# Post-norm with ScalarE's square root and one Newton step, the first side transposed inside the tail, and the S5 tables' sines and copies issued at other places

## The reference

```python
def rmsnorm(x, gain):
    xf = x.astype(jnp.float32)
    y = xf * lax.rsqrt(jnp.mean(xf * xf, axis=-1, keepdims=True) + EPS)
    return (y * gain.astype(jnp.float32)).astype(x.dtype)

    for i in range(DEPTH_2):                 # DEPTH_2 = 2, EPS = 1e-6
        h = rmsnorm(x, mix_pre_gain[i])
        m = fox_mixer(...) if i == 0 else s5_mixer(...)
        x = x + rmsnorm(m, mix_post_gain[i])
        h = rmsnorm(x, ffn_pre_gain[i])
        x = x + rmsnorm(swiglu(h, ffn_w_gate[i], ffn_w_up[i], ffn_w_down[i]), ffn_post_gain[i])
```

## Time and profile before

| | |
|---|---|
| time before, median of 3 runs | 1224.45 us (1222.07 to 1225.02) |
| the profiled execution: time, span | 1224.62 us, 1222.8 us |
| mean granted TensorE clock | 0.976 of full speed |
| PE busy | 1151.2 us, 94% of the span, 7172 instructions |
| DVE busy | 799.1 us, 65% |
| ACT busy | 593.1 us, 49% |
| POOL busy | 117.8 us, 10% |
| DMA | 177.43 MB, mean 145 GB/s |
| the chain that ended last | PE 76%, DVE 13%, ACT 7%, POOL 2% |

### The profile page before, as it was taken

The page is one execution under the profiler, slowest core; times in us unless marked ns, Lnnn a source line. Parts: engine busy times, 40 slices in busy tenths (PEclk is TensorE's granted clock), DMA queues, the critical chain, the costliest instruction groups (busy, mean ns, idle before and its releaser), DMA issues.

```text
span 1222.8 us, 17457 instructions
## 1 busy us (share of the span) xinstructions
PE 1151.2 (94%) x7172; PEld 949.6 (78%) x7172; DVE 799.1 (65%) x1299; ACT 593.1 (49%) x907; POOL 117.8 (10%) x120
## 2 busy tenths in 40 slices
PE   7898799999999999999998899999988898999997
PEld 6766688797888888888777777887877677888785
DVE  5647763547767768555667886778768958455643
ACT  6465322325356656356664664343582256435441
POOL 0304150400000000000000000002304400000000
PEclk9899799999999999999999999999998899999999
DMA  8533012113455555554422554555441143555551
GB/s 304 178 105 95 26 52 70 35 53 131 151 200 173 183 178 173 188 185 164 153 89 98 189 197 160 187 184 190 165 145 54 58 148 137 197 189 187 189 189 52
DMA packets 49664, 177.43 MB, mean 145 GB/s; under 512 B 5648, under 2 KB 6288, under 8 KB 49328
## 3 DMA queue, kind: packets, MB, share of 16 engines
q1 hardware_dynamic: 49584, 176.32, 42.6%
HBM read 175.25 MB, written 1.05 MB: 144 GB/s over the span
## 4 chain that ended last, share of the span: by engine, by line
PE 76%; DVE 13%; ACT 7%; POOL 2%; issue 2%; DMA 1%; SPq 0%; DVEq 0%; ACTq 0%
PE wps L2616 20%; PE wps L2618 20%; PE wps L2617 20%; PE tps L2605 4%; DVE wlo L1773 3%; ACT whi L1390 2%; PE tps L2817 2%; PE tps L2826 1%; PE tps L2839 1%; DVE bt L2379 1%; DVE bt L2390 1%; DVE arena L1998 1%; PE tps L2662 1%; PE tps L3012 1%; POOL arena L2509 1%
## 5 line engine op out<-in xcount | busy, mean ns | idle before, releaser
L1773 DVE TENSOR_TENSOR wlo<-raw,whi 128x1024 fp32r<-128x1024 f32 (+1 forms) x322 | 388.6, 1231 | 184.2 <-ACT whi L1390 182.9
L2616 PE MATMUL wps<-whi,a_hi 128*128 128x512 f32 (+1 forms) x1008 | 405.4, 402 | 19.0 <-DVE a_lo L1795 7.8
L2617 PE MATMUL wps<-whi,a_lo 128*128 128x512 f32 (+1 forms) x1008 | 395.4, 392 | 0.0
L2618 PE MATMUL wps<-wlo,a_hi 128*128 128x512 f32 (+1 forms) x1008 | 395.2, 392 | 0.0
L1390 ACT ACTIVATE whi<-raw 128x1024 fp32r<-128x1024 f32 (+1 forms) x322 | 325.3, 1050 | 53.1 <-PE wps L2618 48.8
L2616 PEld LDWEIGHTS wps<-whi,a_hi 128*128 128x128 f32 x1008 | 192.4, 191 | 64.5 <-DVE wlo L1773 13.8
L2618 PEld LDWEIGHTS wps<-wlo,a_hi 128*128 128x128 f32 x1008 | 192.0, 191 | 40.7
L2617 PEld LDWEIGHTS wps<-whi,a_lo 128*128 128x128 f32 x1008 | 192.5, 191 | 36.4
L2616 PE MATMUL wps<-whi,f_hi 128*128 128x512 f32 x264 | 104.8, 397 | 0.0
L2618 PE MATMUL wps<-wlo,f_hi 128*128 128x512 f32 x264 | 104.3, 395 | 0.0
L2617 PE MATMUL wps<-whi,f_lo 128*128 128x512 f32 x264 | 104.3, 395 | 0.0
(11 more groups left out here) (402 smaller groups left out, 1335.4 us busy)
## 6 DMA issues: line engine op xcount, KB each, us to landing
raw<-in_w_dn SPq DMA_DIRECT2D x22, 512.0 KB, 3.6
raw<-in_w_0dn SPq DMA_DIRECT2D x22, 512.0 KB, 3.6
raw<-in_w_1dn SPq DMA_DIRECT2D x22, 512.0 KB, 4.2
raw<-in_w_ua SPq DMA_DIRECT2D x20, 512.0 KB, 3.6
raw<-in_w_ub SPq DMA_DIRECT2D x20, 512.0 KB, 3.7
raw<-in_w_0ug SPq DMA_DIRECT2D x20, 512.0 KB, 3.6
raw<-in_w_0uu SPq DMA_DIRECT2D x20, 512.0 KB, 3.7
raw<-in_w_1ug SPq DMA_DIRECT2D x20, 512.0 KB, 3.7
```

Source lines behind the costliest of these rows:

```text
L1773: V.tensor_tensor(t.wlo[n % NR][:, 0:w], t.raw[n % NR][:, 0:w], t.whi[n % NH][:, 0:w].bitcast(F32), ALU.subtract).then_inc(m.done(s.dve_lo ...
L2616: T.matmul(o, xh, wh, start=first, stop=False)
L2617: T.matmul(o, xl, wh, start=False, stop=False)
L2618: mm = T.matmul(o, xh, wl, start=False, stop=last)
```

## The change

The post-norm's reciprocal square root is formed in another way. ACT computes the square root of the mean (the first half's sum comes in as a bias that DVE has prepared at place (0,1), the second half's sum is the input), DVE takes the reciprocal of it and does one Newton step. Beside it, an ACT square root of a constant is issued at (0,1), so that the table of the square root is loaded there. In each post-norm all squares now come ahead of the multiplications. Side 0 is turned behind (1,2), inside the tail of the second half's stream, and no longer behind the stream. `b_power` is emitted at one piece per slab from 12 slabs ahead of 0dn0 on, so `s5_angle` and what follows come earlier; the sines are emitted from slab 3 of 0dn0's on instead of 14; the three groups of copies `c_spread` are emitted at the end of the first 7 slabs of 0dn1, at place (0,0) of its tail, and in si0's stream; `local_weights` is spread over one more slab.

```diff
-    def postnorm(names, nk, acts, then=None, begun=None):
+    def postnorm(names, nk, acts, then=None, begun=None, beside_tail=lambda banks: None):
...
+        def biases(banks):
+            for j in range(2):
+                emit("post_bias", i, j)
...
-        banks = whole(stream(names[1], nk, acts, {(0, TAIL - 1): half_way}))
-        take_in(1, 1, banks, first)
+        banks = whole(stream(names[1], nk, acts, {(0, 0): beside_tail, (0, 1): biases, (0, TAIL - 1): half_way, (1, 2): lambda b_: first()}))
+        take_in(1, 1, banks)
...
                 emit("b_power", k, i)
                 yield
-                if at["use"] < down_slab:
+                if at["use"] < down_slab - 12:
                     yield
...
         emit("c_zero")
-        for k in range(3):
-            emit("c_spread", k)
-            yield
+        emit("c_spread", 0)
+
+    def last_spread():
+        emit("c_spread", 2)
+        yield
...
-    sine_slab, dead_slab = down_slab + 14, SLABS.index(("0dn1", 6, 512)) + 1
+    sine_slab, dead_slab = down_slab + 3, SLABS.index(("0dn1", 6, 512)) + 1
-    x4, second = swiglu(0, second, ("mix_pre", 8))
+    x4, second = swiglu(0, second, ("mix_pre", 8), beside_tail=lambda banks: emit("c_spread", 1))
...
                     k_bank[0].held = False
+            else:
+                yield
             yield
...
+    background.append(last_spread())
     background.append(local_weights())
...
     @part
+    def post_bias(i, j):
+        if j == 0:
+            act.wait_ge(*m.at("eps", 3))
+            activate(t.st[:, 54:55], t.eps[:, 0:1], ACT.Sqrt, bias=t.eps[:, 0:1], scale=1.0)...
+
+    @part
+    def post_root(i, j):
+        act.wait_ge(*m.at("post_square", i, 1, j))
+        act.wait_ge(*m.at("post_bias", i, j))
+        activate(t.st[:, 48 + j:49 + j], t.st[:, 41 + 2 * j:42 + 2 * j], ACT.Sqrt, bias=t.st[:, 50 + j:51 + j], scale=1.0 / D)...
...
+    def post_bias(i, j):
+        dve.wait_ge(*m.at("post_square", i, 0, j))
+        V.tensor_scalar(t.st[:, 50 + j:51 + j], t.st[:, 40 + 2 * j:41 + 2 * j], 1.0 / D, 1e-6, ALU.mult, ALU.add)...
...
     def post_root(i, j):
-        a = t.st[:, 44 + j:45 + j]
-        for c in range(2):
-            dve.wait_ge(*m.at("post_square", i, c, j))
+        a, xh, y, tt = (t.st[:, c + j:c + j + 1] for c in (44, 52, 48, 56))
+        dve.wait_ge(*m.at("post_square", i, 1, j))
         V.tensor_tensor(a, t.st[:, 40 + 2 * j:41 + 2 * j], t.st[:, 41 + 2 * j:42 + 2 * j], ALU.add)...
-        after_last()
-        rsqrt(t.st[:, 46 + j:47 + j], a, 1, 1.0 / D, 1e-6, "post_root", i, j)
+        V.tensor_scalar(xh, a, -0.5 / D, -0.5e-6, ALU.mult, ALU.add)...
+        dve.wait_ge(*m.at("post_sqrt", i, j))
+        V.reciprocal(y, y)...
+        V.scalar_tensor_tensor(tt, y, y, xh, ALU.mult, ALU.mult)...
+        V.scalar_tensor_tensor(t.st[:, 46 + j:47 + j], tt, 1.5, y, ALU.add, ALU.mult)...
```

More of the change, by code:

```diff
@@ L732, in postnorm, with take_in @@
         done = [[(("post", i, c, j),) for c in range(2)] for j in range(2)]
-        def take_in(c, j, banks, between=None):
+        def take_in(c, j, banks):
             b = banks[j]
[L736 to L744, removed]
+            emit("post_square", i, names[c], c, j, b.name)
+            emit("post_times", i, names[c], c, j, b.name)
+            b.free = (("post_times", i, c, j),)
         def close(j):
@@ L764, in postnorm, with swiglu @@
         return done, second
-    def swiglu(l, second, then=None):
+    def swiglu(l, second, then=None, **more):
         ffn = Acts(f"f{l + 1}")
@@ L791, in swiglu @@
         to_acts("sg1", [("gate_up", name, j) for j in range(2)], ffn, 2, k0=20)
-        return postnorm([f"{l}dn0", f"{l}dn1"], 22, ffn, then)
+        return postnorm([f"{l}dn0", f"{l}dn1"], 22, ffn, then, **more)
     emit("fox_start", x2_all)
@@ L1610, in post_square @@
         last_square[:] = [("post_square", i, c, j)]
+    @part
+    def post_bias(i, j):
+        if j == 0:
+            act.wait_ge(*m.at("eps", 3))
+            activate(t.st[:, 54:55], t.eps[:, 0:1], ACT.Sqrt, bias=t.eps[:, 0:1], scale=1.0).then_inc(m.done(s.act_out, "root_table", i), 1)
+    @part
+    def post_root(i, j):
+        act.wait_ge(*m.at("post_square", i, 1, j))
+        act.wait_ge(*m.at("post_bias", i, j))
+        activate(t.st[:, 48 + j:49 + j], t.st[:, 41 + 2 * j:42 + 2 * j], ACT.Sqrt, bias=t.st[:, 50 + j:51 + j], scale=1.0 / D).then_inc(
+            m.done(s.act_out, "post_sqrt", i, j), 1)
     @part
@@ L2131, in post_times @@
         dve.wait_ge(*m.at("post_gain", i))
-        if after_square:
-            dve.wait_ge(*m.at("post_square", i, c, j))
+        dve.wait_ge(*m.at("post_square", i, c, j))
         V.tensor_tensor(t.h[:, j, cols], t.bank[b][:, :], t.gain[:, cols], ALU.mult).then_inc(m.done(s.dve_out, "post_times", i, c, j), 1)
     @part
+    def post_bias(i, j):
+        dve.wait_ge(*m.at("post_square", i, 0, j))
+        V.tensor_scalar(t.st[:, 50 + j:51 + j], t.st[:, 40 + 2 * j:41 + 2 * j], 1.0 / D, 1e-6, ALU.mult, ALU.add).then_inc(
+            m.done(s.dve_out, "post_bias", i, j), 1)
+    @part
     def post_root(i, j):
-        a = t.st[:, 44 + j:45 + j]
-        for c in range(2):
-            dve.wait_ge(*m.at("post_square", i, c, j))
+        a, xh, y, tt = (t.st[:, c + j:c + j + 1] for c in (44, 52, 48, 56))
+        dve.wait_ge(*m.at("post_square", i, 1, j))
         V.tensor_tensor(a, t.st[:, 40 + 2 * j:41 + 2 * j], t.st[:, 41 + 2 * j:42 + 2 * j], ALU.add).then_inc(m.done(s.dve_out, "post_sum", i, j), 1)
-        after_last()
-        rsqrt(t.st[:, 46 + j:47 + j], a, 1, 1.0 / D, 1e-6, "post_root", i, j)
+        dve.wait_ge(*m.at("post_sum", i, j))
+        V.tensor_scalar(xh, a, -0.5 / D, -0.5e-6, ALU.mult, ALU.add).then_inc(m.done(s.dve_out, "post_half", i, j), 1)
+        dve.wait_ge(*m.at("post_sqrt", i, j))
+        V.reciprocal(y, y).then_inc(m.done(s.dve_out, "post_guess", i, j), 1)
+        dve.wait_ge(*m.at("post_guess", i, j))
+        V.scalar_tensor_tensor(tt, y, y, xh, ALU.mult, ALU.mult).then_inc(m.done(s.dve_out, "post_error", i, j), 1)
+        dve.wait_ge(*m.at("post_error", i, j))
+        V.scalar_tensor_tensor(t.st[:, 46 + j:47 + j], tt, 1.5, y, ALU.add, ALU.mult).then_inc(m.done(s.dve_out, "post_root", i, j), 1)
     @part
```

6 lines of the change are left out of this document (2 added, 4 removed).

## The result

The changed kernel takes 1217.45 us, the median of 5 runs (1216.00 to 1217.96), against 1225.02 us for the kernel before on the same chip (5 runs, 1222.07 to 1227.67). The ratio is 0.9933, 95% interval 0.9912 to 0.9953. The forecast was 1218.5 (1215.0 to 1222.5).

The account below looks back on a forecast made before the run. PE, busy 94% of the span, bounds the kernel; time is only in its waits and behind its last matmul. −4.6 − 1.6 + 1.4 − 1.8 − 0.54 + 1.0 = −6.1 us gives 1218.5, range 1215.0 to 1222.5.

Parts of the forecast that it names:

- The chain: Post-norm, from sum to first addition to x: the sum and four operations take 0.95 us, 1.55 less than before.
- fo and so: The post-norms behind fo and so: 2.3 us gained at each, together −4.6 us.
- The end: Behind the last matmul: the additions start 1.6 us earlier with nothing to hide it, −1.6 us.
- A: At 0ut: DVE stands behind POOL at s5_angle's first operation, so the up products start later; +1.4 us.
- rivals 1 and 2: Rival 1: moved S5 work gives the gains back, 1229.6, chance 0.06; rival 2: one or two clock falls, 1221.5, chance 0.22.
- B: 0dn1 to si0: PE goes on at 896.85 instead of 898.65, −1.8 us; the copies behind are gone, −0.54.
- C: si0 to si1: PE must wait at h's transposes; +1.0 us, between 0 and 2.
- the fall at 893.5: Lower granted clock, 0.51, over nine matmuls after the 2.65 us wait; assumed to go with it, part of the −1.8.
- The rest of S5: The S5 work behind si1 and the drive: the forecast sum had no term for it.
- Rival 3: Each table load costs 1.38 us more as a drain of ACT's queue, PE waits 1.2 at three post-norms; 1222.1, chance 0.05.

Follow-up runs that it names:

- turn_late: The changed kernel with side 0 turned behind the stream as before, not inside the tail; 1217.88 us, ratio 0.9930 to the kernel before.
- old_queue: turn_late with DVE's multiplication of side 1 ahead of a_lo again and ACT's square behind it; 1218.00 us, ratio 0.9935.
- angle_later: The changed kernel with s5_angle held back by about one slab; 1214.52 us, ratio 0.9913 to the kernel before.
- keep_busy: The changed kernel with PE's wait for h at 0ut filled with 20 transposes whose result is overwritten; 1221.72 us, ratio 0.9970.
- again: The changed kernel itself, run once more beside its variants; 1217.70 us, ratio 0.9939 to the kernel before.
- tables_only: The kernel before with only the S5 tables' work at its new places and the old post-norm; 1232.61 us, ratio 1.0039.
- three_steps: The changed kernel with the old root of 13 operations on DVE and no table load; 1224.62 us, ratio 0.9992.
- copies_behind: angle_later with the second group of copies issued behind side 0's square and root in 0dn1's tail; 1214.51 us, ratio 0.9910.
- no_fetch: The changed kernel without the dummy square root at (0,1), so the root loads its own table; 1220.46 us, ratio 0.9952.

## Why the prediction was right, step by step

- **The chain**, 0.95 us: 0.90. The square root hides, as said, though it takes 0.29 us and not 0.23 at most; the reciprocal takes 0.16 us, no more than its neighbours.
- **fo and so**, −2.3 each: −2.36 and −2.55. The working took the gain from side 1's queue, not from side 0's turn, and that is what bounds it. What it did not say is that the turn has no part in it. Its picture of the wait for a_lo, that PE had turned side 0 and could not begin the next stream, stood for a cause, and what PE waited for was DVE's queue of root, additions, two splits and a multiplication: turn_late and old_queue show that.
- **The end**, −1.6: −1.74.
- **A**, +1.4: +1.36, by the mechanism named. The clock's fall of rivals 1 and 2 came behind it, +1.55 by angle_later and keep_busy. It was not in the sum.
- **B and C**, −1.8 − 0.54 + 1.0 = −1.34: B and C measured +0.15 with that fall, −1.4 without it. Singly, without it: B −2.1 for −1.8, C +0.68 for +0.46. Some 1.7 of B's 2.1 is the fall at 893.5 that goes; the prediction had assumed that it goes and had called it a part. ACT's square was late as said, PE waited 1.18 us for x (1.3 said) and 0.34 at side 1. C's waits came at other places than said: 0.40 us for h, and 0.83 ahead of the drive, which I had not seen.
- **The rest of S5** stood at 0 and measured −2.58 (−2.00 in again). This term was missing. It is the clock: 3.4 us less were lost in 934 to 986, of which waits gave some back. The runs bear that out: tables_only, three_steps and copies_behind, which lose 8.5 to 9.1 us of clock in this stretch as the kernel before does (8.5), have −0.14 to −0.26 here, the others, with 3.4 to 7.1, have −1.65 to −2.58. Why the falls are shorter in some kernels and not in others is open, and copies_behind, a variant of the changed kernel, does not have this gain.
- **Rival 3**: no drain, at 678.40 and at 683.02 the next activation starts 0.02 and 0.01 us behind the load's end. 26 loads against 22, each 1.28 us. The Trainium skill, "ScalarE: Activation LUTs", section "What ACT_TABLE_LOAD costs", has 1283 ns for the load, which these traces show too, and about 1380 ns of drain, which they don't.

So −6.1 became −7.1 in the profiles. The single terms of waiting were good to 0.3 us. That the sum is near as well is partly luck: two terms of the clock that were not in it, +1.55 and −2.58, cancel in large part, and the 0.51 us that the profiled execution was late at its start offset the 0.5 us by which the waiting terms gained more than said.

## What to carry to other kernels

Before a wait is put down to the piece that ends it, read what stood in that engine's queue: here, of a PE wait for a_lo of 2.30 us, 0.97 went with a norm's small operations and 0.58 with a multiplication moved behind a_lo, 0.75 stayed, and turning earlier gave nothing. When an engine is lent to other work, look at who stands behind the first operation that can wait: one operation of s5_angle cost 1.4 us directly and 1.5 us by the clock. And where a kernel loses 5 to 17 us to the clock, a local gain below 2 us has to be read at its place in the trace; the median of the whole says little on it. The best versions here are angle_later and copies_behind, 1214.5 us, 3 below the changed kernel.

## What the runs showed of the chip

- The granted clock fell behind PE's wait of 2.4 us at 0ut in 6 of the 8 profiled kernels that have it, and in none of the 6 that wait 1.05 us or fill the wait. In these runs the fall needed the standing, but the same wait of 2.41 us went without a fall in three_steps and old_queue. Which other condition decides is open. A fall there costs 1.5 us.
- A fall that begins in the drive, 256 matmuls of 64 columns, lasted 13.7 us and cost 4.6 us to the drive's end, with no wait inside it. The wait for h behind it takes up a part of the rest (2.32 us in no_fetch, 4.10 in the changed kernel).
- Executions of one kernel form two groups 7 to 9 us apart (keep_busy, tables_only), at mean clocks of about 0.98 and 0.97. That the fall in the drive makes the difference is likely, and not shown: the profiled execution is of the longer group in both kernels.
- A square root of one column on ACT takes 0.29 us, a reciprocal of one column on DVE 0.16 us.
